# Five stage boundaries of a two-block transformer kernel without a meeting of all engines

## The chip, the cores and the metric

The kernel runs on one core of a Trainium2 chip. The metric is the device time of one launch in microseconds, the median over runs. Everything is float32.

## The reference, cut to what matters

512 tokens (four tiles of 128) of width 1024 go through two blocks. The first block mixes (gMLP, RG-LRU, HGRN2, pooling), then a convolved feed-forward, then a gated per-layer embedding. The second block has attention and routed experts, two layers of it.

```python
# first block, one layer (D_MODEL 1024, D_FF 2816)
h = rms_norm(x, norm1_g); z = h @ w_in; mix = concat(y_a, y_b, y_c, y_d)
x = x + mix @ w_out                                   # stage mix_out
hf = causal_dwconv(rms_norm(x, norm2_g) @ w_up)       # stage up
gt, val = split(hf)
x = x + (gelu(gt) * val) @ w_down                     # stage down
gate = sigmoid(rms_norm(x, norm3_g) @ w_pg)           # stage gate
x = rms_norm(x + (p @ w_pe) * gate, final_g)
# second block, two layers
x = layer_norm(ALPHA * x + mixer(x), ...)             # even_in, even_ab, even_out / odd_in ... odd_out
x = layer_norm(ALPHA * x + routed_moe(x), ...)        # route, experts, overflow, combine
```

## The kernel before, in words

The five engines run one list of 22 stages, `STAGES`. At the end of a stage each engine calls `meet()`: it drains, adds one to the semaphore `met` and waits until all four compute engines have done so. The stages named in `NO_MEET` (line 194) leave this out; before, those are the output projections, the routing and the experts of the second block. So the PE, DVE, ACT and POOL programs of every other stage start together. Semaphores for products and evacuations belong to a `Flow`; two of them take turns by the stage's parity, and POOL clears the one of the stage that ended.

Five of the stage ends that meet matter here: mix_out to up, up to down, down to gate, gate to even_in, combine0 to odd_in.

**Weights.** They come in pieces of up to 2 MB into `ring`, six slots, issued in order by SP. SP waits for `w_used`, which PE raises by `release()` when a piece has been used, so that the next five pieces are there or on the way. `product()` (line 579) is a chain of matmuls over the eight 128-row pieces of the contraction. Each float32 matmul of the program is two PE instructions in the trace, each with a weight load of its own, so a 128 x 512 product over the full width is 16 instructions.

**The end of an output stage** (mix_out, down, gate). PE computes two column halves for the four token tiles. DVE adds each into `x` (`residual()`), and after the second half of a tile it computes the norm's statistics (`norm_tile()`), with a square root by ACT, and writes the normalised tile. PE turns the tile, eight transposes of 128 x 128 (`turn_tile()`, line 586), into two PSUM banks, and the tile is copied from there into `xT`, the operand of the next stage: by DVE with a gain for mix_out and down (`take_tile`, line 1655), by ACT for gate (line 1211), by both for combine0 (`take`, lines 1257 and 2210). `turn_behind()` (line 606) turns a tile two products behind; after the last product three tiles are turned one after the other, and for mix_out and down tile 3 waits for the banks of tile 1. In combine(), all four turns come after the last product. DVE's order in `residual()` is: norm of tile 2, take tile 0, norm of tile 3, take tiles 1, 2, 3.

**The stages behind them.** `up()` (line 804) makes 44 feature products with `xT` (512 columns) as the moving operand; ACT scales each into `conv`, DVE adds the two other taps, and the last 22 are multiplied into `hidden`. `down()` (line 817) reads `hidden` as the stationary operand, six pieces, eight banks. `gate()` (line 836) makes for each tile and half a product with `pT` (4 instructions) and one with `xT` (16), in pairs of banks. `even_in()` (line 862) and `odd_in()` (line 1085) begin with feature products over all of `xT`.

**POOL.** In `up()` it clears the rows of `expert_rows` with 12 writes of 512 KB (line 2358) and waits for them; in `down()` it loads `pT`, in `gate()` the gain `final_g` and the pack for even_in; in `odd_in()` it clears halves of `kI`.

## Time and profile before

| | us |
|---|---|
| median of 3 timed runs | 2092.29 |
| lowest, highest | 2090.55, 2104.61 |
| the profiled execution | 2081.75 |
| its span on the core | 2080.1 |

The profile shows the profiled execution alone. Its span is the time from the first to the last instruction; 1.65 us lie around it. Start times in the rows below are microseconds from the start of the span. In the timeline a row is a run of like instructions: start, time that it covers, engine, line and operation, output and input with their sizes, count, and in brackets the idle time of the engine before it with what ended it.

### The profile page before, as it was taken

The page shows a single profiled execution, that of the slowest core. Times are in us where ns is not written, and L with a number is a line of the kernel's source. Part 1 is how long each engine was busy: PE and PEld are TensorE (multiplying, and loading weights), DVE is VectorE, ACT ScalarE, POOL GpSimd, SP SyncE. Part 2 cuts the span into 40 slices and gives each one's busy share as a digit, 9 for nine tenths or more (in the row PEclk, how much of TensorE's full clock was granted, in tenths as well). Part 3 has the DMA queues.
Part 4 walks back from the last instruction along what each step waited for, and adds up shares of the span by engine and source line. Part 5 has one row for each costly group of instructions (what it writes and reads, how often), then busy time and mean ns, then how long its engine had stood idle before and what let it go on. Part 6 is the DMA issues. An engine that isn't in the chain of part 4 may idle for free.

```text
span 2080.1 us, 23209 instructions
## 1 busy us (share of the span) xinstructions
PE 1960.8 (94%) x9718; PEld 886.6 (43%) x9718; DVE 671.1 (32%) x1600; ACT 401.1 (19%) x869; POOL 82.3 (4%) x106
## 2 busy tenths in 40 slices
PE   6999999999999998999996999998999898899997
PEld 3464444444444444444644333333645445333332
DVE  3746322223300033014725100005686645300005
ACT  3203011111100003103701111112116431111112
POOL 0000010000000000000000200010000000200001
PEclk9989999999999999999996999999898998899999
DMA  4203552211221113101044899992110234599994
GB/s 151 71 21 103 199 203 81 74 51 67 81 81 61 61 54 121 64 18 41 1 162 148 310 424 414 416 388 114 41 41 1 81 122 162 171 415 417 420 412 188
DMA packets 71001, 335.56 MB, mean 161 GB/s; under 512 B 4536, under 2 KB 12744, under 8 KB 58480
## 3 DMA queue, kind: packets, MB, share of 16 engines
q1 hardware_dynamic: 56752, 283.80, 35.4%
q0 software_dynamic: 10976, 37.76, 4.8%
q10 hardware_dynamic: 3168, 12.50, 1.5%
q8 instruction: 78, 1.28, 0.2%
q14 instruction: 27, 0.22, 0.0%
HBM read 310.94 MB, written 23.09 MB: 161 GB/s over the span
## 4 chain that ended last, share of the span: by engine, by line
PE 90%; DVE 5%; ACT 2%; issue 1%; DMA 1%; DVEq 0%; another core or an unknown queue 0%; ACTq 0%; SPq 0%
PE psum L582 39%; PE psum L983 24%; PE psum L825 7%; PE psum L762 4%; PE psum L894 3%; PE psum L923 2%; PE psum L907 2%; PE psum L965 1%; PE psum L1078 1%; PE psum L1009 1%; PE psum L704 1%; PE psum L594 1%; ACT ring L1436 1%; PE psum L1101 0%; PE psum L658 0%
## 5 line engine op out<-in xcount | busy, mean ns | idle before, releaser
L983 PE MATMUL psum<-ring,scratch 128*32 128x512 f32 x3840 | 507.8, 598 | 2.9 <-DVE scratch L2139 1.6
L582 PE MATMUL psum<-xT,ring 128*128 128x512 f32 (+2 forms) x1056 | 466.0, 602 | 8.6 <-PE psum L582 3.4
L582 PEld LDWEIGHTS psum<-xT,ring 128*128 128x128 f32 (+2 forms) x1056 | 199.7, 191 | 272.4 <-issue 271.5
L983 PEld LDWEIGHTS psum<-ring,scratch 128*32 128x32 f32 x3840 | 140.6, 111 | 285.0 <-issue 276.5
L582 PE MATMUL psum<-ring,xT 128*128 128x512 f32 (+4 forms) x704 | 242.6, 501 | 2.5 <-ACTq L1187 1.6
L582 PEld LDWEIGHTS psum<-ring,xT 128*128 128x128 f32 x704 | 123.1, 199 | 120.1 <-issue 111.9
L825 PE MATMUL psum<-ring,scratch 128*128 128x512 f32 x352 | 155.7, 603 | 4.0 <-remote 3.3
L1600 DVE SCALAR_TENSOR_TENSOR scratch<-psum,overlay,scratch 128x511 f32<-128x511 f32 x88 | 65.9, 749 | 232.2 <-ACT scratch L1366 230.6
L983 PE MATMUL psum<-xT,scratch 128*32 128x512 f32 x768 | 127.0, 593 | 0.0
L2137 DVE TENSOR_TENSOR scratch<-psum,scratch 128x512 f32<-128x512 f32 x24 | 16.6, 692 | 309.9 <-PE psum L983 309.9
L825 PEld LDWEIGHTS psum<-ring,scratch 128*128 128x128 f32 x352 | 67.4, 193 | 91.6 <-issue 91.6
L762 PE MATMUL psum<-xT,ring 128*128 128x512 f32 x224 | 101.6, 609 | 2.5 <-DVEq L1589 2.3
L1600 DVE SCALAR_TENSOR_TENSOR x<-x,psum 128x512 f32<-128x512 f32 x32 | 22.0, 688 | 234.7 <-PE psum L825 141.3
L1366 ACT ACTIVATE scratch<-psum,overlay 128x512 f32<-128x512 f32 x44 | 34.2, 778 | 269.5 <-PE psum L582 269.5
L582 PE MATMUL psum<-ring,scratch 128*128 128x512 f32 x160 | 72.6, 606 | 3.0 <-DVEq L1589 1.6
L2139 DVE COPY scratch<-psum 128x512 f32<-128x512 f32 x24 | 16.6, 692 | 179.8 <-PE psum L1009 179.8
L894 PE MATMUL psum<-scratch 64*128 64x256 f32 (+11 forms) x256 | 68.1, 483 | 4.0 <-DVEq L1589 1.8
L1424 ACT ACTIVATE ring<-ring,small 128x257 f32<-128x257 f32 (+5 forms) x128 | 68.1, 540 | 6.3 <-DVE small L1990 6.3
L1210 ACT ACTIVATE small<-small 128x1 f32<-128x1 f32 x20 | 4.1, 203 | 337.5 <-DVE small L1636 337.5
L762 PEld LDWEIGHTS psum<-xT,ring 128*128 128x128 f32 x224 | 43.5, 196 | 55.5 <-issue 55.2
L1458 ACT ACTIVATE scratch<-psum 128x512 f32<-128x512 f32 x48 | 26.3, 595 | 191.5 <-PE psum L965 191.5
L1483 ACT ACTIVATE scratch<-psum 128x512 f32<-128x512 f32 x48 | 28.7, 597 | 155.7 <-PE psum L983 155.7
(374 smaller groups left out, 1667.1 us busy)
## 6 DMA issues: line engine op xcount, KB each, us to landing
ring<-in_moe_w_gate SPq DMA_DIRECT2D x28, 2048.0 KB, 11.0
ring<-in_moe_w_up SPq DMA_DIRECT2D x28, 2048.0 KB, 13.6
ring<-in_moe_w_down SPq DMA_DIRECT2D x24, 2048.0 KB, 12.4
ring<-in_w_up SPq DMA_DIRECT2D x11, 2048.0 KB, 7.9
xT<-in_moe_w_down SPq DMA_DIRECT2D x8, 2048.0 KB, 11.6
expert_rows<-scratch ACTq DMA_DIRECT2D x20, 512.0 KB, 10.9
ring<-in_w_down SPq DMA_DIRECT2D x4, 2048.0 KB, 7.7
ring<-in_even_w_in SPq DMA_DIRECT2D x4, 2048.0 KB, 7.7
```

What stands on the lines that cost most here:

```text
L582: mm = nc.tensor.matmul(out_, lhsT, rhs, start=(j == 0), stop=(j == len(pairs) - 1))
L762: mm = nc.tensor.matmul(banks[k % 2][:, :], lhsT, rhs, start=(t == 0), stop=(t == KD - 1))
L825: mm = nc.tensor.matmul(banks[4 * half_ + n][:, :], hidden[:, k0 + t, n * P:(n + 1) * P], w_[:, t, :], start=(k0 + t == 0), stop=(k0 + t = ...
L894: mm = nc.tensor.matmul(banks[2 * (p % 2) + hh][:, 0:span(kind, n)[1]], head_q(kind, n, j, hh), head_k(kind, n, j, hh), start=True, stop=True)
L907: mm = nc.tensor.transpose(banks[4 + u % 2][:, b * P:(b + 1) * P], probs[:, u % 6, b * P:(b + 1) * P], ident)
L923: mm = nc.tensor.matmul(banks[6 + g % 2][r, c], head_v(kind, s0 // P + b, h), probsT[:, (2 * p + hh) % 4, b * P:(b + 1) * P], start=(b == ...
L983: mm = nc.tensor.matmul(bank[r, :], lhsT[:, t, r], w_[:, t, c0:c0 + 512], start=(t == 0), stop=(t == nk - 1))
L1366: A(conv[:, k % 4, :], banks[k % 8][:, :], ACT.Identity, bias=operand["fconv_b"][:, k:k + 1], scale=w3[:, k, 2:3]).then_inc(f.a, 1)
L1424: A(to, of, ACT.Exp, bias=negmax[:, u % 8:u % 8 + 1], accum_out=p_total[:, u % 8:u % 8 + 1])\
L1458: A(xgT[:, 4 * h:4 * h + 4, :].rearrange("p a b -> p (a b)"), banks[h][:, :], ACT.Copy).then_inc(xgT_ready, 1)
L1483: A(y_sb[:, g % 2, j * 512:(j + 1) * 512], banks[5 + j][:, :], ACT.Copy).then_inc(y_taken, 1)
L1600: return V.scalar_tensor_tensor(out_, in0, s, in1, ALU.mult, ALU.add)
```

## The change

The five stages mix_out, up, down, gate and combine0 join `NO_MEET`, so there is no meeting at the five boundaries. Data waits take its place:

- The output stages share one product counter `out_mm` and one evacuation counter `out_used` with base values; gate has counters of its own; `Flow`s are given to five stages, and POOL clears them after norm1 and even_in.
- At the three boundaries into feature products (up, even_in, odd_in), the last tile is turned no longer by the stage before. A new function `enter_features()` waits for tiles 0 to 2, multiplies their 384 columns for the first feature, turns tile 3, multiplies the 384 columns for the second feature, waits for tile 3, and then multiplies the remaining 128 columns for both.
- gate waits for each tile when it needs it, uses the banks in a rotated order (`gate_bank`: 4, 6, 0, 2), and turns the last tile of down after its first pair of products.
- down waits for the eviction of up's last banks bank by bank and for `hidden` piece by piece (`val_scaled`).
- POOL's steps of these stages run as soon as their own waits allow: the clearing writes of up() right after the meeting of mixers, the load of `pT` behind them. `final_g` waits for down's last product, the pack for even_in for the last tile taken, the clearing of `kI` for the last product of combine0.
- The expert pieces count in `w_loaded` instead of semaphores of their own (not shown). Sizes and order of the loads stay as they are.

```diff
@@ -191,7 +191,7 @@
-NO_MEET = ("even_out", "route0", "experts0", "overflow0", "odd_out", "route1", "experts1", "overflow1")
+NO_MEET = ("mix_out", "up", "down", "gate", "combine0", "even_out", "route0", "experts0", "overflow0", "odd_out", "route1", "experts1", "overflow1")
@@ -279,7 +280,14 @@
                 self.mm, self.a, self.v, self.s = (sem(f"{name}_{m}") for m in ("mm", "act", "dve", "stats"))
         turns = [Flow("even_stage"), Flow("odd_stage")]
-        flow = {s: turns[i % 2] for i, s in enumerate(STAGES)}
+        flow = {"norm1": turns[0], "up": turns[1], "even_in": turns[0], "odd_in": turns[1], "latent": turns[0]}
+        done_with = {"norm1": turns[0:1], "even_in": turns}
+        gate_mm, gate_opened, gate_used = sem("gate_mm"), sem("gate_opened"), sem("gate_used")
+        out_mm, out_used = sem("out_mm"), sem("out_used")
+        OUT_MM = {"mix_out": 0, "down": 8, "even_out": 32, "odd_out": 40}
+        OUT_USED = {"mix_out": 0, "down": 8, "even_out": 16, "odd_out": 24}
...
         late_w, late_mm, late_ready, late_done = sem("late_w"), sem("late_mm"), sem("late_ready"), sem("late_done")
+        late_taken = sem("late_taken")
         early_added, over_known, moe_rows = sem("early_added"), sem("over_known"), sem("moe_rows")
@@ -470,7 +482,14 @@
         def turn_bank(stage, n):
-            return 2 * n if stage in ("gate", "combine0") else 2 * (n % 2)
+            if stage == "gate":
+                return gate_bank(n)
+            return 2 * n if stage == "combine0" else 2 * (n % 2)
+        def gate_bank(i):
+            return (2 * i + 4) % 8
         keys_cleared = sem("keys_cleared")
         listed = sem("listed")
@@ -610,10 +629,34 @@
                 if n == NT - 1:
                     route_tile(stage, n - 3)
                     turn_tile(stage, n - 1)
+                    if stage in ("mix_out", "down", "gate"):
+                        return
                     route_tile(stage, n - 2)
                     route_tile(stage, n - 1)
                     turn_tile(stage, n)
                     route_tile(stage, n)
+            def tile_there(stage, n):
+                pe.wait_ge(tile_taken, norm_base[stage] + n + 1)
+                if stage == "combine0":
+                    pe.wait_ge(late_taken, n + 1)
+            def enter_features(behind, f, columns):
+                def part(k, q):
+                    w_, c0, m = columns[k]
+                    return product(banks[k][0:m, q], [(w_[:, t, c0:c0 + m], xT[:, t, q]) for t in range(KD)])
+                early, last = slice(0, (NT - 1) * P), slice((NT - 1) * P, T)
+                tile_there(behind, NT - 2)
+                part(0, early)
+                turn_tile(behind, NT - 1)
+                part(1, early)
+                tile_there(behind, NT - 1)
+                for k in range(2):
+                    part(k, last).then_inc(f.mm, 1)
@@ -783,20 +826,19 @@
             def halves(name, chunk_name, lhs):
-                f = F[name]
                 for half_, (at, c) in enumerate(by_name[chunk_name]):
                     arrived(at)
                     w_ = slot_view(at, c)
                     for n in range(NT):
                         k = NT * half_ + n
                         product(banks[k][:, :], [(lhs[:, t, n * P:(n + 1) * P], w_[:, t, :]) for t in range(KD)])\
-                            .then_inc(f.mm, 1)
+                            .then_inc(out_mm, 1)
                         if half_ == 1:
                             if n == NT - 1:
@@ -806,7 +848,9 @@
                 for j, (at, c) in enumerate(by_name["w_up"]):
                     arrived(at)
                     w_ = slot_view(at, c)
-                    for g in range(4):
+                    if j == 0:
+                        enter_features("mix_out", f, [(w_, g * P, P) for g in range(2)])
+                    for g in range(0 if j else 2, 4):
                         k = 4 * j + g
                         if k >= 8:
@@ -815,25 +859,27 @@
                     release(f.mm, 4 * j + 4)
             def down():
-                f = F["down"]
                 for j, (at, c) in enumerate(by_name["w_down"]):
                     arrived(at)
                     w_ = slot_view(at, c)
                     half_, k0 = j // 3, c[1]
+                    pe.wait_ge(val_scaled, k0 + c[2])
                     for n in range(NT):
+                        if j == 0:
+                            pe.wait_ge(F["up"].v, 2 * FT - 3 + n)
                         for t in range(c[2]):
                             mm = nc.tensor.matmul(banks[4 * half_ + n][:, :], hidden[:, k0 + t, n * P:(n + 1) * P],
                                                   w_[:, t, :], start=(k0 + t == 0), stop=(k0 + t == FT - 1))
-                        mm.then_inc(f.mm, 1)
+                        mm.then_inc(out_mm, 1)
...
                         if j == 5:
                             if n == NT - 1:
-                                release(f.mm, NT * 6)
+                                release(out_mm, OUT_MM["down"] + NT * 6)
                             turn_behind("down", n)
                     if j < 5:
-                        release(f.mm, NT * (j + 1))
+                        release(out_mm, OUT_MM["down"] + NT * (j + 1))
             def gate():
-                f = F["gate"]
@@ -842,34 +888,41 @@
                     arrived(at)
                     w_g = slot_view(at, c)
                     for n in range(NT):
-                        k = 2 * (NT * half_ + n)
-                        bank_emptied(f, "va" * 8, k)
-                        product(banks[k % 8][:, :], [(pT[:, t, n * P:(n + 1) * P],
-                                                      w_e[:, t, half_ * 512:(half_ + 1) * 512]) for t in range(2)])\
-                            .then_inc(f.mm, 1)
-                        bank_emptied(f, "va" * 8, k + 1)
-                        product(banks[(k + 1) % 8][:, :], [(xT[:, t, n * P:(n + 1) * P], w_g[:, t, :]) for t in range(KD)])\
-                            .then_inc(f.mm, 1)
+                        i = NT * half_ + n
+                        if half_ == 0:
+                            tile_there("down", n)
+                        else:
+                            pe.wait_ge(gate_used, i - NT + 1)
+                        product(banks[gate_bank(i)][:, :], [(pT[:, t, n * P:(n + 1) * P],
+                                                             w_e[:, t, half_ * 512:(half_ + 1) * 512]) for t in range(2)])
+                        product(banks[gate_bank(i) + 1][:, :], [(xT[:, t, n * P:(n + 1) * P], w_g[:, t, :]) for t in range(KD)])\
+                            .then_inc(gate_mm, 1)
+                        if i == 0:
+                            turn_tile("down", NT - 1)
                         if half_ == 1:
                             if n == NT - 1:
-                                release(f.mm, 16)
-                                release(f.mm, 16)
+                                release(gate_mm, 8)
+                                release(gate_mm, 8)
                             turn_behind("gate", n)
                     if half_ == 0:
-                        release(f.mm, 8)
+                        release(gate_mm, NT)
             def even_in():
                 f, k = F["even_in"], 0
                 pe.wait_ge(pack_loaded["even"], 16)
                 for j, (at, c) in enumerate(by_name["even_w_in_2"]):
                     arrived(at)
+                    if j == 0:
...
+                        enter_features("gate", f, [(slot_view(at, c), g * P, P) for g in range(2)])
+                        k = 2
                     if j == 1:
                         bank_emptied(f, EVEN_IN, k)
                         product(banks[k % 8][0:8, :], [(fg_w[:, t, :], xT[:, t, :]) for t in range(KD)]).then_inc(f.mm, 1)
                         k += 1
                         features(f, EVEN_IN, k, at, c, 0)
                         k += 1
-                    for g in range(4):
+                    for g in range(0 if j else 2, 4):
@@ -1079,7 +1132,7 @@
                                                   y_sb[:, g, h * 512:(h + 1) * 512], start=(g == 0), stop=(g == 1))
                     mm.then_inc(late_done, 1)
                 if l == 0:
-                    for n in range(NT):
+                    for n in range(NT - 1):
                         turn_tile("combine0", n)
             def odd_in():
@@ -1087,8 +1140,8 @@
                 (a0, c0), (a1_, c1), (a2, c2) = by_name["odd_w_in_2"]
                 pe.wait_ge(pack_loaded["odd"], 16)
                 arrived(a0)
-                features(f, ODD_IN, 0, a0, c0, 384, HD)
-                features(f, ODD_IN, 1, a0, c0, P)
+                w_ = slot_view(a0, c0)
+                enter_features("combine0", f, [(w_, 384, HD), (w_, P, P)])
                 features(f, ODD_IN, 2, a0, c0, 2 * P)
                 for n in range(NT):
@@ -1663,16 +1714,15 @@
             def residual(name, scale, loads=0, first=None):
-                f = F[name]
                 for k in range(10):
                     if first and k < NT:
                         first(k)
                     if k < 8:
-                        dve.wait_ge(f.mm, (20 if k >= 4 else 8) + k % 4 + 1 if name == "down" else k + 1)
+                        dve.wait_ge(out_mm, OUT_MM[name] + ((20 if k >= 4 else 8) + k % 4 + 1 if name == "down" else k + 1))
                         r = x[:, k % 4, (k // 4) * 512:(k // 4 + 1) * 512]
-                        mul_add(r, r, scale, banks[k][:, :]).then_inc(f.v, 1)
+                        mul_add(r, r, scale, banks[k][:, :]).then_inc(out_used, 1)
                         if k >= 4:
@@ -2210,8 +2259,9 @@
                 def take(n):
                     dve.wait_ge(tile_turned, base + n + 1)
                     for k in range(KD // 2, KD):
-                        V.tensor_scalar(xT[:, k, n * P:(n + 1) * P], banks[2 * n + 1][:, (k - 4) * P:(k - 3) * P],
-                                        operand["moe_g"][:, k:k + 1], operand["moe_b"][:, k:k + 1], ALU.mult, ALU.add)
+                        ins = V.tensor_scalar(xT[:, k, n * P:(n + 1) * P], banks[2 * n + 1][:, (k - 4) * P:(k - 3) * P],
+                                              operand["moe_g"][:, k:k + 1], operand["moe_b"][:, k:k + 1], ALU.mult, ALU.add)
+                    ins.then_inc(late_taken, 1)
                 for n in range(NT + 2):
@@ -2330,13 +2380,12 @@
             steps = [2]
-            def meet(i):
+            def meet(stage):
                 meets[0] += 1
                 pool.drain().then_inc(met, 1)
                 pool.wait_ge(met, 4 * meets[0])
                 pool.drain()
-                if i >= 0:
-                    f = turns[i % 2]
+                for f in done_with.get(stage, ()):
                     for s in (f.mm, f.a, f.v, f.s):
                         pool.sem_clear(s)
@@ -2375,7 +2424,10 @@
                 pool.dma_start(pT.rearrange("p t q -> p (t q)"), w["pT"]).then_inc(pT_loaded, 16)
             def gate():
+                pool.wait_ge(out_mm, OUT_MM["down"] + 24)
                 pool.dma_start(rowsG, w["final_g"]).then_inc(rows_loaded, 16)
+                pool.wait_ge(tile_taken, norm_base["down"] + NT)
                 pool.dma_start(pack_area["even"], w["pack_even"]).then_inc(pack_loaded["even"], 16)
             def clear_halves(tiles):
@@ -2390,6 +2442,8 @@
                 pool.dma_start(kB[HD:HD + 1, :, :], negc[0:8, :]).then_inc(bias_row, 16)
             def odd_in():
+                pool.wait_ge(late_done, NT)
                 clear_halves(kI)
```

## Rows read from the trace of the kernel before

**Rows 1.** The page's first part and its clock row.

```profile
PE 1960.8 (94%) x9718; PEld 886.6 (43%) x9718; DVE 671.1 (32%) x1600; ACT 401.1 (19%) x869; POOL 82.3 (4%) x106
...
PEclk9989999999999999999996999999898998899999
```

**Rows 2.** The chain of work that ended last, shares of the span by engine.

```profile
PE 90%; DVE 5%; ACT 2%; issue 1%; DMA 1%; DVEq 0%; another core or an unknown queue 0%; ACTq 0%; SPq 0%
```

**Rows 3.** Pieces of that chain in order: start us, us, what, instructions.

```profile
577.71 3.27 another core or an unknown queue
580.98 30.79 PE psum L825 x64
611.91 27.72 PE psum L825 x64
...
746.63 36.75 PE psum L582 x80
```

**Rows 4.** Stretches: busy us (instructions) of each engine, granted clock, DMA share, GB/s.

```profile
578.00:580.00 2.00, 0.00 (x0) 0.00 (x0) 1.40 (x2) 0.53 (x1) 0.00 (x0) 1.00 0.47 87
...
582.00:584.00 2.00, 2.00 (x4) 0.97 (x3) 0.00 (x0) 0.23 (x1) 0.27 (x1) 0.50 1.15 375
...
588.00:590.00 2.00, 2.00 (x6) 0.94 (x5) 0.00 (x0) 0.00 (x0) 0.00 (x0) 1.00 0.03 8
```

**Rows 5.** Timeline, mix_out to up.

```profile
259.07 1.94 PE L594 MATMUL psum<-base,scratch 128*128 128x128 f32 x16
...
262.93 3.82 DVE L1659 TENSOR_TENSOR xT<-psum,overlay 128x512 f32<-128x512 f32 x6
...
266.90 2.07 PE L582 MATMUL psum<-xT,ring 128*128 128x512 f32 x2 [1.48 <-DVEq L1589]
```

**Rows 6.** Timeline, up to down.

```profile
580.13 0.69 DVE L1922 TENSOR_TENSOR scratch<-scratch 128x512 f32<-128x512 f32 x1
```

**Rows 7.** Timeline, down to gate.

```profile
738.32 1.94 PE L594 MATMUL psum<-base,scratch 128*128 128x128 f32 x16
...
745.07 1.29 DVE L1659 TENSOR_TENSOR xT<-psum,overlay 128x512 f32<-128x512 f32 x2 [0.41 <-PE psum L594]
...
746.63 3.75 PE L582 MATMUL psum<-ring,scratch 128*128 128x512 f32 x4 [1.60 <-DVEq L1589]
```

**Rows 8.** Timeline, gate to even_in.

```profile
819.45 1.94 PE L594 MATMUL psum<-base,x 128*128 128x128 f32 x16 [0.30 <-PE psum L582]
...
823.52 2.04 ACT L1215 ACTIVATE xT<-psum 128x512 f32<-128x512 f32 x4
...
827.85 4.61 PE L582 MATMUL psum<-xT,ring 128*128 128x512 f32 x5 [1.38 <-ACTq L1187]
```

**Rows 9.** Timeline, combine0 to odd_in.

```profile
1429.23 1.09 PE L594 MATMUL psum<-base,x 128*128 128x128 f32 x8 [2.83 <-DVE x L2205]
...
1429.77 2.88 ACT L1261 ACTIVATE xT<-psum,base 128x128 f32<-128x128 f32 x8
...
1435.19 5.35 PE L582 MATMUL psum<-xT,ring 128*64 128x512 f32 x6 [1.80 <-ACTq L1187]
```

**Rows 10.** Timeline, transposes between products, and products of 128 columns.

```profile
251.02 1.04 PE L594 MATMUL psum<-base,scratch 128*128 128x128 f32 x8
...
251.89 7.03 PE L582 MATMUL psum<-ring,scratch 128*128 128x512 f32 x16
...
872.14 7.31 PE L582 MATMUL psum<-ring,xT 128*128 128x128 f32 x64
```

**Rows 11.** The page's costliest groups: busy, mean ns of one, idle before.

```profile
L582 PEld LDWEIGHTS psum<-ring,xT 128*128 128x128 f32 x704 | 123.1, 199 | 120.1 <-issue 111.9
```

**Rows 12.** Timeline of SP's issues, and stretches of mix_out with columns as in Rows 4.

```profile
202.38 95.82 SPq L2525 DMA_DIRECT2D ring<-in_w_up  x7
...
210.00:220.00 10.00, 10.00 (x25) 4.42 (x24) 1.00 (x2) 0.00 (x0) 0.00 (x0) 1.00 1.05 387
...
240.00:250.00 10.00, 10.00 (x25) 4.42 (x24) 4.77 (x12) 0.41 (x2) 0.00 (x0) 1.00 0.00 0
```

40 lines of the change are left out of this document (20 added, 20 removed).

## The prediction

> **What bounds the kernel now.** I read the page's busy shares first. TensorE is busy for 1960.8 of 2080.1 us, and its clock row stands at 9 or nearly 9 everywhere except in a few slices [rows 1]. The chain of work that ended last says the same from the other side: 90% of it is PE [rows 2]. So only time in which PE stands still, or runs at the lower level of its clock, can be won, and a faster DVE or DMA is worth nothing by itself. The next view is the same chain in order of time, because there a hole in PE's work shows as a piece that is not PE. At the end of up there is such a hole of 3.27 us, and the 64 instructions behind it take 30.79 us, while the next 64, of the same kind, take 27.72 [rows 3]. The third view, stretches of 2 us, tells why: granted clock 1.00 while PE stands still, 0.50 from 582 to 584, 1.00 again from 588 [rows 4]. That is 2.4 GHz, then 1.2 GHz, then 2.4 GHz. A hole therefore costs twice, once as idle time and once as slow work behind it. The last view is the timeline of each of the five boundaries, to see what PE waits for [rows 5 to 9].
>
> **What the meetings cost themselves.** Almost nothing. Before up, DVE's last copy into xT ends at 262.93 + 3.82 = 266.75, and PE starts at 266.90: 0.15 us [rows 5]. Before gate it is 746.63 - (745.07 + 1.29) = 0.27 us [rows 7]. So the gain is not five meetings, it is what PE can do before the last tile of xT exists. This has to be counted boundary by boundary. The unit prices: one full instruction 27.72 / 64 = 0.433 us [rows 3]; one of 384 columns 0.75 of it, 0.325; one of 128 columns 7.31 / 64 = 0.114 [rows 10]; eight transposes between products 251.89 - 251.02 = 0.87 us [rows 10].
>
> **1. up to down.** PE is idle from 577.71 to 580.98. ACT and DVE work in it on up's last feature; the last step, the product into hidden, ends at 580.13 + 0.69 = 580.82 [rows 6]. After the change down's first piece needs features 0 to 7 of hidden and the banks of features 40 to 43, one by one; the last of those banks is asked for after three groups of 16 instructions, 21 us later, and the last feature only in the third piece. So PE goes on after the usual step between pieces, 611.91 - (580.98 + 30.79) = 0.14 us [rows 3]. Gain 3.27 - 0.14 = 3.13, and without a hole the clock has no reason to fall: 30.79 - 27.72 = 3.07. Together **6.20 us**. The cover of ACT's and DVE's tail is down's first 21 us; without it, it costs again the 3.1.
>
> **2. down to gate.** The transposes of tiles 1 and 2 end at 738.32 + 1.94 = 740.26; gate begins at 746.63 [rows 7]. After the change gate's first pair (4 + 16 instructions, 8.7 us) needs only tile 0, which has been taken long before, and banks 4 and 5, emptied long before. It starts at 740.26 + 0.15. Tile 3's transposes follow it, at about 749, when its banks have long been free; its copy (1.3 us) ends before the fourth pair asks for it, 17 us later. DVE waits for those transposes with its gate work queued behind them, but the first sigmoid is there only at 749 as well, and the pairs leave 8.7 us for each. Gain 746.63 - 740.41 = 6.22, less 0.87 for transposes that now stand in the line of work: 5.35. The 80 instructions from 746.63 took 36.75 us, at the full clock 80 x 0.433 = 34.65 [rows 3]: 2.10 more. Together **7.45 us**.
>
> **3. mix_out to up.** PE can start when tile 2 is taken, but DVE takes tiles 1, 2, 3 in one go of 3.82 us, 1.27 each, after the norm of tile 3. Tile 2 is there at 262.93 + 2.55 = 265.48, so PE starts at 265.63 and wins 1.27 us, no more. It now carries tile 3's transposes itself: 0.87. The two features cost 32 x 0.325 + 32 x 0.114 = 14.05 us instead of 32 x 0.433 = 13.86: 0.19. DVE's copy of tile 3 lies beside the second 384-column part (5.2 us). PE's idle stretch from 261.01 to 265.63 is no shorter than before, so I leave the slow stretch behind it as it is. Left: **0.21 us**.
>
> **4. gate to even_in.** The same with ACT taking the tiles: tiles 1 and 2 are there at 823.52 + 2.04 = 825.56, PE starts at 825.71 instead of 827.85 [rows 8]. 2.14 - 0.87 - 0.19 = **1.08 us**, slow stretch kept.
>
> **5. combine0 to odd_in.** Tiles 1 and 2 are taken at 1429.77 + 2.88 = 1432.65, start at 1432.80 instead of 1435.19 [rows 9]: 2.39 - 0.87 - 0.19 = **1.33 us**, slow stretch kept.
>
> **What I cost at nothing.** The counters out_mm and gate_mm replace others one for one. POOL's pT, final_g and even_in pack are asked for by POOL as soon as their places are free, and each is needed tens of us later. Clearing kI moves from odd_in into combine0, beside DVE's chain there; at worst two memsets' worth, about 1 us. The clearing writes, 12 x 512 KB = 6.3 MB, move from up to mix_out, past the w_up pieces that SP has queued from 202.38. There the DMA engines moved 387 GB/s from 210 to 220 and nothing from 240 to 250 [rows 12]. 6.3 MB at 387 GB/s are 16 us and end by about 250, before up asks for its first piece at 265.6. The Trainium skill (Trainium Kernel Development and Optimization, Key Constraints) says that transfers from SP's, ACT's and POOL's queues run on the same 16 DMA engines and interleave; so moving these writes would not be free of the loads. The row of 210 to 220 with share 1.05 agrees that nothing is to spare there; by the rule alone the sum stays the same as long as the idle stretch behind it holds both.
>
> **The sum.** 6.20 + 7.45 + 0.21 + 1.08 + 1.33 = 16.3 us. Against the profiled execution: 2081.75 - 16.3 = 2065.5. That execution lies 0.5% under the median of the timed runs, 2092.29, and a gain of a fixed number of us should not depend on it, so the forecast is 2092.3 - 16.3 = **2076.0 us**, 0.8% less.
>
> **Unknown costs, from both sides.** (a) The slow stretch at boundaries 3 to 5. Where it can be read it cost 2.10 and 3.07 us [rows 3]. It may vanish at all three (up to 3 x 3.07 = 9.2 more gain) or catch tile 3's transposes and a longer part (about 1 us more at each). The Trainium skill (TensorE: Matmul & The Clock Gate, Part 1) says that the same kernel has differing numbers of slow matmuls from run to run; that is a reason for a range and gives no other sum. (b) The 3 x 32 = 96 narrow instructions. The nearest row has a stationary operand of the same size and 128 columns, 0.114 us [rows 10]; the other bound is the length of a weight load, 199 ns [rows 11], should it not hide under so short a matmul: 96 x 0.085 = 8.2 more. I take 0.114, because weights are loaded in that row as well. (c) The median of three runs: the runs of before lie 14 us apart, so a median may be off by 6 to 8.
>
> **Rivals.**
> - *The clock doesn't fall at boundaries 3 to 5 any more.* For it: two of the three holes get shorter. Against: the transposes that broke the hole before are now behind it, so the hole in one piece is longer at boundary 3 (4.6 us against 3.2, from 261.01 to the copy of tile 1 at 264.20). Gain 16.3 + 9.2 = 25.5: 2066.8 us. Chance 0.12.
> - *The narrow pieces are bound by their weight loads*, as in (b): gain 8.1, 2084.2 us. Against: 64 such instructions in a row at 0.114. Chance 0.08.
> - *The clock still falls at boundaries 1 and 2*, for instance because the step between stages is longer than thought: gain 16.3 - 5.2 = 11.1, 2081.2 us. Chance 0.05.
> - *The change does not do what it says*: the gain is given back later, where loads and not PE set the pace, in the experts' stages. For it: the DMA share there is high. Against: PE is 90% of the chain over the whole span, and the loads wait for PE's releases. 2091 us. Chance 0.04.
> - *Slower: the clearing writes hold up the weights.* Place: mix_out, where 6.3 MB of writes share the engines with the second w_out piece and the first w_up piece, 4.2 MB. Those 10.5 MB must be through by 265.6, 63 us after 202.4: 166 GB/s suffice, 387 were seen. Each us later costs PE one. It decides from 80 us on, that is below 131 GB/s, where the delay eats the 16.3; at a quarter of the measured rate, 97 GB/s, the writes end at 310.6, 45 us late: 2121 us. Chance 0.03.
> - The forecast: 0.68.
>
> **The range.** 2065 to 2088: down to the first rival, up past the second and third, with the spread of a median of three on either side. What a measurement of this kernel can tell from no change is about 1%, 21 us: below 2071.4 or above 2113.2. Faster by that: the first rival, and of the forecast, whose centre is 4.6 us short of the bound, about a fifth: 0.12 + 0.13 = 0.25. Slower by it: the last rival, 0.03. The rest is 0.72.
>
> **What would show it.** Step 1: no hole at the end of up, down's first 64 instructions in 27.7 us, granted clock 1.00 throughout. Step 2: the first gate product within 0.3 us of the transposes, 80 instructions and 8 transposes in 35.5 us. Steps 3 to 5: PE starts right after tile 2's copy, and the 32 narrow instructions take 3.7 us. For the last rival: PE waiting for DMA in mix_out or up. The prediction is wrong if the clock falls in a place where PE had no hole, if the narrow instructions take over 0.15 us each, or if any stage behind shows an idle time of PE that it had not before.

## The result, and the profile after

| | us |
|---|---|
| kernel before, median of 4 runs (lowest, highest) | 2095.91 (2090.55, 2104.61) |
| changed kernel, median of 4 runs (lowest, highest) | 2074.22 (2069.86, 2079.25) |
| ratio after / before, 95% interval | 0.9893 [0.9849, 0.9937] |
| profiled execution, before and after | 2081.75, 2074.65 |
| span, before and after | 2080.1, 2073.0 |

The forecast was 2076.0. The medians differ by 21.7 us, the two profiled executions only by 7.1. Both differences have to be explained; neither is the 16.3 of the sum. The forecast took its start from a median of three runs of the kernel before, 2092.3; with the fourth run beside the result it is 2095.9.

The page after, its first part and its clock row, answers to [rows 1], and its chain by engine to [rows 2].

```profile
PE 1960.0 (95%) x9814; PEld 895.2 (43%) x9814; DVE 670.9 (32%) x1600; ACT 401.0 (19%) x869; POOL 82.1 (4%) x106
...
PEclk9989999999999999999996999999989997999999
...
PE 91%; DVE 4%; ACT 2%; issue 1%; DMA 1%; DVEq 0%; SPq 0%; ACTq 0%
```

96 more PE instructions, as counted; PE is still the bound. The page is too coarse for a gain of 1%, so I went to the chain of the changed kernel in order of time: start us, us, what, instructions.

```profile
265.52 7.09 PE psum L601 x16
272.61 0.87 PE psum L613 x8
273.48 22.48 PE psum L601 x80
...
548.20 27.72 PE psum L601 x64
576.21 27.72 PE psum L872 x64
604.22 27.72 PE psum L872 x64
...
731.26 1.94 PE psum L613 x16
733.20 8.59 PE psum L601 x20
741.78 0.87 PE psum L613 x8
742.66 25.77 PE psum L601 x60
...
808.62 1.95 ACT xT L1268 x4
810.71 7.92 PE psum L601 x16
```

Against [rows 3]: between up's last 64 instructions, which end at 575.92, and down's first at 576.21 only a step of 0.29 us is left, and down's first 64 instructions take 27.72 instead of 30.79. From down's transposes (731.26) to gate (733.20) there is no hole either; tile 3's eight transposes stand behind the first 20 instructions. At the entry of up and of even_in the first piece of 16 is one of 384 columns. The stretches of 2 us answer to [rows 4] (busy us and instructions of PE, PEld, DVE, ACT, POOL; granted clock; DMA share; GB/s).

```profile
262.00:264.00 2.00, 0.00 (x0) 0.00 (x0) 1.94 (x4) 0.00 (x0) 0.00 (x0) 1.00 1.04 404
...
266.00:268.00 2.00, 2.00 (x5) 1.08 (x4) 0.00 (x0) 0.00 (x0) 0.00 (x0) 0.57 0.04 11
268.00:270.00 2.00, 2.00 (x5) 1.14 (x4) 0.00 (x0) 0.00 (x0) 0.00 (x0) 0.58 0.00 0
270.00:272.00 2.00, 2.00 (x8) 1.20 (x7) 0.00 (x0) 0.00 (x0) 0.00 (x0) 1.00 0.00 0
...
578.00:580.00 2.00, 2.00 (x6) 0.95 (x5) 0.98 (x2) 0.02 (x1) 0.00 (x0) 1.00 0.99 354
580.00:582.00 2.00, 2.00 (x6) 0.90 (x5) 0.00 (x0) 0.00 (x0) 0.00 (x0) 1.00 0.98 377
```

At up to down the clock stays at 2.4 GHz; at mix_out to up it still falls to 1.2 GHz, with the hole that was left there.

**The stretch table.** To compare many profiles I took the starts of PE's instructions in each trace and the time between fixed ones: from mix_out's first product to up's third feature (A), from there to down's second piece (B), from there to the second half of gate (C), from there to even_in's third feature (D), and from combine0's first product to odd_in's third feature (E). Each holds exactly one of the five boundaries. The last column is the rest, from odd_in's third feature to the end. The rows are all profiles of the two kernels; the padded ones are described below.

| us | A | B | C | D | E | rest |
|---|---|---|---|---|---|---|
| before | 81.35 | 328.10 | 171.79 | 60.47 | 41.12 | 628.30 |
| before_again | 79.66 | 326.68 | 171.75 | 60.46 | 41.39 | 631.47 |
| before_third | 81.31 | 328.07 | 171.76 | 60.46 | 40.24 | 638.94 |
| before_p192 (padded) | 80.83 | 324.98 | 172.89 | 60.74 | 41.41 | 631.51 |
| before_route (padded) | 82.09 | 327.99 | 171.75 | 60.47 | 38.37 | 629.85 |
| mean | 81.05 | 327.16 | 171.99 | 60.52 | 40.51 | |
| after | 79.62 | 322.17 | 164.49 | 59.37 | 39.72 | 633.21 |
| after_again | 79.62 | 322.16 | 164.49 | 59.34 | 39.82 | 626.68 |
| after_third | 79.62 | 322.17 | 164.50 | 59.35 | 39.33 | 630.81 |
| after_p64 (padded) | 80.29 | 322.20 | 164.50 | 59.32 | 39.84 | 626.69 |
| after_p128 (padded) | 80.76 | 322.19 | 164.55 | 59.54 | 39.76 | 626.70 |
| after_route64 (padded) | 79.62 | 322.19 | 164.49 | 59.30 | 39.31 | 626.26 |
| mean | 79.92 | 322.18 | 164.50 | 59.37 | 39.63 | |
| first pair's gain | 1.73 | 5.93 | 7.30 | 1.10 | 1.40 | -4.91 |
| gain of the means | 1.13 | 4.98 | 7.49 | 1.15 | 0.88 | |
| the prediction | 0.21 | 6.20 | 7.45 | 1.08 | 1.33 | |

What lies ahead of A and between D and E, where PE's instructions are the same in both kernels, is not in the table. The five stretches gained 1.73 + 5.93 + 7.30 + 1.10 + 1.40 = 17.5 us in the first pair and 15.6 in the means; the sum of the prediction was 16.3. B and C lie clear of the spread of either kernel, and so does D. A and E do not: before_again has an A of 79.66 and before_route an E of 38.37. What remains is why the first pair shows 7.1 and the medians about 20.

### The profile page after: what moved, and what is told of

Read it like the earlier page. It is cut to its first block, busy times and chain, and to the rows that moved or that the text cites. A ratio compares the mean times of both kernels' runs of the same rounds, so it can differ in the third digit from the quotient of the medians.

```text
span 2073.0 us, 23327 instructions
## 1 busy us (share of the span) xinstructions
PE 1960.0 (95%) x9814; PEld 895.2 (43%) x9814; DVE 670.9 (32%) x1600; ACT 401.0 (19%) x869; POOL 82.1 (4%) x106
## 4 chain that ended last, share of the span: by engine, by line
PE 91%; DVE 4%; ACT 2%; issue 1%; DMA 1%; DVEq 0%; SPq 0%; ACTq 0%
PE psum L601 39%; PE psum L1036 25%; PE psum L872 7%; PE psum L805 5%; PE psum L947 3%; PE psum L976 2%; PE psum L960 2%; PE psum L1018 1%; PE psum L1131 1%; PE psum L1062 1%; PE psum L747 1%; PE psum L613 1%; ACT ring L1487 1%; PE psum L1154 0%; PE psum L701 0%
## 5 line engine op out<-in xcount | busy, mean ns | idle before, releaser
L1036 PE MATMUL psum<-ring,scratch 128*32 128x512 f32 x3840 | 518.4, 598 | 5.3 <-DVE scratch L2188 1.6
L601 PE MATMUL psum<-xT,ring 128*128 128x512 f32 (+5 forms) x1152 | 465.3, 564 | 15.3 <-DVE xT L1710 4.5
L601 PEld LDWEIGHTS psum<-xT,ring 128*128 128x128 f32 (+2 forms) x1152 | 210.1, 190 | 266.1 <-issue 257.1
L872 PE MATMUL psum<-ring,scratch 128*128 128x512 f32 x352 | 152.7, 593 | 1.8 <-PE psum L872 1.5
L601 PE MATMUL psum<-ring,scratch 128*128 128x512 f32 x160 | 70.7, 594 | 1.3 <-ACTq L1240 0.9
## 6 DMA issues: line engine op xcount, KB each, us to landing
ring<-in_moe_w_gate SPq DMA_DIRECT2D x28, 2048.0 KB, 10.9
```

The lines of the kernel that those rows point to most:

```text
L601: mm = nc.tensor.matmul(out_, lhsT, rhs, start=(j == 0), stop=(j == len(pairs) - 1))
L872: mm = nc.tensor.matmul(banks[4 * half_ + n][:, :], hidden[:, k0 + t, n * P:(n + 1) * P], w_[:, t, :], start=(k0 + t == 0), stop=(k0 + t = ...
L1036: mm = nc.tensor.matmul(bank[r, :], lhsT[:, t, r], w_[:, t, c0:c0 + 512], start=(t == 0), stop=(t == nk - 1))
```

## The experiments

There are three sets of runs, each with its own runs of the kernel before beside it on one chip. The theory was that the five stretches give the gain, by PE's work in the holes and by the clock behind the two that close. One rival was that the missing meetings give it by themselves. Another was that part of the gain is given back in the experts' stages, as the first profile after seemed to show.

### What the first profile gave back

This is a piece of the chain of the changed kernel in the experts' stage of the first layer, 128 instructions of hidden products.

```profile
1137.90 7.67 PE psum L1036 x64
1145.57 0.39 issue
1145.96 1.31 PE psum L1036 x4
1147.27 0.12 issue
1147.39 7.07 PE psum L1036 x60
1154.46 1.09 PE psum L1018 x8
```

The 128 instructions take 1154.46 - 1137.90 = 16.56 us, and PE waits for nothing that the profile shows. The four at 1145.96 take 0.33 us each instead of 0.11, and the granted clock is 1.00 (stretches, columns as before):

```profile
1146.00:1148.00 2.00, 1.88 (x12) 0.47 (x15) 0.00 (x0) 0.37 (x1) 0.00 (x0) 1.00 0.01 0
1148.00:1150.00 2.00, 2.00 (x24) 0.69 (x18) 0.00 (x0) 0.22 (x1) 1.56 (x2) 1.00 0.94 82
```

There are two such places in each layer's experts. By PE's starts the same instructions take 2.7, 3.8, 2.7 and 3.8 us more than in before, 13.0 together. That is what the first pair gave back: 17.5 less 13.0, and 2.6 won elsewhere by the clock, make 7.1. Two things lay near the places in that profile: a train of eight indexed transfers that POOL issues one after the other, and a boundary between two pieces in which PE's program is fetched (the page's instruction queue for it moves 79 packets after, 78 before). The change moves PE's instructions against these pieces, so my theory was that it had brought a boundary into the train of transfers. Waits that hold at once, put into PE's program, shift the boundaries.

```diff
+            for _ in range(128):      # after_p64: 64 more PE instructions; after_p128: 256 waits, 128;
+                pe.wait_ge(root_set, 1)   # before_p192: 384 waits, 192. All ahead of the first stage
             for s in stages:
```

> The changed kernel with 64 more semaphore instructions at the very start of PE's program (a wait on root_set that is long fulfilled), where PE waits for x anyway, so that they cost nothing themselves. The change made PE's program 192 instructions longer in front of the experts, and PE's program is fetched in pieces of 256 instructions (16 KB packets of the instruction queue); 64 more bring the edges of these pieces back to where they were before. Theory 1, that the four slow places of PE in the experts' stages (together about 13 us in the profile of the changed kernel) come from piece edges that fall late into POOL's train of eight indirect DMAs: the four places are gone, the span is 2073.0 - 13 = 2060. Rival, that they come from the changed times or from the new semaphores: they stay, 2073.

> The kernel before with 192 more semaphore instructions at the start of PE's program, under 10 us at 0.05 us each, while PE waits until 13 us for x: by themselves about nothing. They put the edges of PE's instruction pieces where the changed kernel has them. Theory 1: the four slow places appear, 2080.1 + 13 = 2093 span, about 0.6% slower than the kernel before. Rival: no change, ratio 1.000 within 0.3%.

> The changed kernel with 128 more semaphore instructions at the start of PE's program. The edges of the pieces come 128 instructions, about 7 us in the experts' stages, earlier than in the changed kernel, so just ahead of the start of POOL's trains or 1 us into them. Theory 1: no slow place in the experts' first groups, span about 2060 to 2066. Rival: 2073.

> The kernel before, unchanged, for a second profile. If its timed runs (2090 to 2105) differ from its profiled one (2081.75) by slow places that come and go, this profile shows some of them; if the profile again gives about 2080 without slow places in the experts, the difference lies elsewhere. Both theories: ratio 1.00.

Measured: after_p64 2065.03 us, ratio 0.9905 [0.9885, 0.9925]; after_p128 2065.64, 0.9923 [0.9901, 0.9944]; before_p192 2095.02, 1.0044 [1.0026, 1.0063]; before_again 2082.54, 1.0006 [0.9992, 1.002]. The slow places were gone in both padded versions of after, but they did not appear in before_p192. It is slower for another reason: its padding is not hidden. PE starts at 21.93 instead of 13.17 us, 8.8 later, and the mixers take 193.0 instead of 189.3. So I moved the padding to a place where PE waits anyway, the routing, and ran the changed kernel again without any.

```diff
+                for _ in range((128, 0)[l]):      # after_route64, ahead of the wait for the choice, layer l
+                    pe.wait_ge(root_set, 1)       # before_route: 160 and 96 in layer 0, 128 in layer 1
```

> The changed kernel, unchanged, beside the others of this chip. Theory 1 (the places of PE's instruction stream decide over the slow places in the experts' stages): the four slow places are there again, first distance of the hidden products 19.8 us instead of 17.2 and last distance 25 instead of 22.64 in both layers, ratio 0.9965 (7 us less). Rival (they come and go by chance): no or other slow places, ratio 0.992.

> The changed kernel with 64 more semaphore instructions of PE (3.3 us) in route0, where PE waits 6.2 us for DVE's choice. So nothing in front of the experts changes, neither instructions nor times. Theory 1: the slow places are gone in both layers, 2073.0 - 12.9 = 2060 span, ratio to the kernel before 0.990 to 0.992, which beats both kernels. Rival: same as the changed kernel, slow places stay.

> The kernel before with 128 more semaphore instructions of PE in route0 (80 where it waits 6.2 us, 48 where it waits 2.9 us) and 64 in route1: exactly so many that the pieces of PE's program end at the same instructions of both experts' stages as in the changed kernel, with the times in front as before. They cost under 1 us. Theory 1: slow places appear in the experts' stages, up to 13 us, ratio 1.006. If the clock time of the edges relative to other traffic matters as well: only some, 1.001 to 1.005. Rival: none, 1.000.

Measured: after_again 2065.12 us, 0.9902 [0.9873, 0.9932]; after_route64 2061.23, 0.9893 [0.9872, 0.9914]; before_route 2084.49, 0.9997 [0.998, 1.0014]. The theory fell. after_again is the changed kernel with nothing altered, and the same 128 instructions stand in one piece:

```profile
1143.29 13.87 PE psum L1036 x128
1157.15 1.09 PE psum L1018 x8
```

13.87 us instead of 16.56. The boundaries of its program are those of the first profile. And before_route, padded so that its pieces meet the train as in after, has no slow place. A last pair of profiles, on one chip, settled whose they are.

> The changed kernel once more, beside the two versions above and the kernel before on one chip. If the net gain is the sum of the five stretches (15 to 17 us) and what the clock does in odd_in and odd_d (2 to 6 us), the ratio is 0.990 to 0.992. The slow places of PE in the experts' stages, 2 to 3 us each, four in the first profile of this kernel and none in the second: if they belong to the program, they are here again; if they come and go between executions, there is no reason to expect any. After odd_in's third feature 626.7 us without them, 633 with four.

> The kernel before, one more profile. Two things were seen in only one of two profiles of it: the stretch at the lower clock behind up's hole, 6.8 us or less (stretch to down's second piece 328.1 or 326.7), and a stretch of 10.2 us at the lower clock in odd_d, costing 4.7 us, which its first profile lacks and the later ones have. If the first is a matter of the execution, the stretch lies between 325 and 328.5; if the second is the rule for this kernel, odd_in's third feature to the end is 631.5, else 628.3.

Measured: after_third 2073.23 us, ratio 0.9918 [0.9886, 0.995]; before_third, a single run, 2096.0 beside a median of 2090.7. Both have slow places, at the same four points of the work: 1.7, 3.6, 1.7 and 2.9 us in before_third, 1.8, 2.7, 1.7 and 2.8 in after_third. The chain of before_third at the first:

```profile
1159.93 2.14 PE psum L983 x18
1162.07 0.10 issue
1162.17 1.06 PE psum L983 x5
1163.23 0.37 issue
1163.60 6.22 PE psum L983 x53
```

The same row of after_third is 0.36 issue between 5 and 54 instructions. The distance from DVE's step on this expert's hidden product to its step on the next is 18.91 us in before_third and 18.93 in after_third, against 17.20 in the profiles without a slow place and 19.86 in the first profile after. The two versions of the next part, profiled on the same chip, have 18.91 and 18.90. So the slow places are a matter of the chip or the moment, not of the change: all four profiles of this set have them, of four different programs, and of the ten others only the first profile after. What they lie next to can be read from the same traces. The first indexed transfer and the slow place behind it stand as follows (us): after 1135.94 and 1145.57, after_third 1138.44 and 1148.25, before_third 1152.26 and 1162.07, 9.6, 9.8 and 9.8 apart, at the eighth transfer of the train.

```profile
1152.26 1.01 POOL L2416 DMA_INDIRECT expert_tokens<-token_id,place  x1 [17.18 <-PE psum L965]
...
1161.31 0.97 POOL L2416 DMA_INDIRECT expert_tokens<-token_id,place  x1 [0.30 <-issue]
```

The nearest packet of PE's program is no such mark: it comes 4.0 us ahead of the place in before_third (1158.1), and 4.3 us behind it in after_third (1152.6). So a fixed distance to the fetching of PE's program is out. The distance to POOL's train does not prove the train, though. A product of PE releases it, and in all fourteen profiles the same instructions of PE run beside it. What sets the five apart is when the train lands. POOL's next transfer waits for it, in after and in after_again:

```profile
1148.14 1.02 POOL L2473 DMA_DIRECT2D idx_sb<-expert_tokens  x1 [2.19 <-DMA expert_tokens<-token_id,place]
```

```profile
1160.90 1.02 POOL L2473 DMA_DIRECT2D idx_sb<-expert_tokens  x1 [9.57 <-DMA expert_tokens<-token_id,place]
```

In both layers this wait is 2.2 to 5.8 us in the five profiles with slow places and 8.7 to 10.9 in the nine without. The slow places thus come with a train that lands sooner. Which of the two brings the other, or what third thing brings both, stays open.

### Each boundary by itself

```diff
-NO_MEET = ("even_out", "route0", "experts0", "overflow0", "odd_out", "route1", "experts1", "overflow1")
+NO_MEET = ("up", "even_out", "route0", "experts0", "overflow0", "odd_out", "route1", "experts1", "overflow1")
...
             def down():
                 f = F["down"]
+                pe.wait_ge(pool_step, 1)
...
+                    pe.wait_ge(val_scaled, k0 + c[2])
                     for n in range(NT):
+                        if j == 0:
+                            pe.wait_ge(F["up"].v, 2 * FT - 3 + n)
```

This is before_up, the kernel before with the one meeting of up taken away and the data waits of the change in its place, and one wait for POOL's first step; gate's counters start from where up's end (not shown).

> The kernel before with the meeting between up and down alone taken away (with the waits that the change puts into down, and one wait of PE on POOL's first step). My sum: 3.13 us of idle time and 3.07 us of slow clock go, 6.2 us in this stretch. By trace after the change this stretch gained 5.9. Rival, that the join pays only together with the others: 0 to 3. The program is shorter or longer by a few instructions only, so no slow places in the experts' stages: ratio 0.997.

Measured: 2083.2 us, 0.9995 [0.9977, 1.0012]. The stretches: A 79.67, B 322.27, C 172.40, D 60.47, E 41.38, rest 631.55. B is within 0.1 us of the changed kernel's; the others, but for C, are those of before. Its stretches of 2 us at the boundary, and its chain:

```profile
576.00:578.00 2.00, 1.61 (x4) 0.87 (x5) 1.14 (x2) 1.97 (x2) 0.00 (x0) 1.00 0.31 61
578.00:580.00 2.00, 2.00 (x6) 0.86 (x5) 1.05 (x2) 0.09 (x1) 0.00 (x0) 1.00 1.01 336
```

```profile
576.39 27.72 PE psum L829 x64
604.11 0.29 issue
604.40 27.72 PE psum L829 x64
```

So step 1 stands alone: hole and slow stretch go with this one meeting. C is 0.6 longer than in before, because each later piece of down carries a second wait, and the step between pieces is 0.29 us instead of 0.14. Against the mean of before, B is 4.9 shorter. So the profile leads one to expect 4.9 - 0.6 = 4.3 us less than the kernel before; the ratio gives 1 us less with an interval from 4.8 us less to 2.5 more. So the gain of this step is shown in the profile and not in the timed runs.

```diff
 # after_gate_late, in gate(): tile 3 turned and awaited before the first pair, not behind it
                         i = NT * half_ + n
+                        if i == 0:
+                            turn_tile("down", NT - 1)
+                            tile_there("down", NT - 1)
                         if half_ == 0:
...
-                        if i == 0:
-                            turn_tile("down", NT - 1)
```

> The changed kernel with one step moved: tile 3 of down's output is turned and awaited before gate's first pair of products and not behind it, without a meeting. Theory (step 2): what is won there is PE's work in the hole, so the hole comes back, 5.35 us, and with it a stretch at the lower clock, about 2.1 us: the stretch from down's second piece to gate's second half goes from 164.5 to about 171.8 us, the kernel is 7.4 us slower than the changed one. Rival: the meeting itself was the cost; then 164.5 stays within 0.5 us. A third case, hole without slow clock: 169.9. All expect the other stretches unchanged (79.6, 322.2, 59.3, 39.8).

Measured: 2083.19 us, 0.9969 [0.9952, 0.9985]; beside after_third on the same chip 10.0 us slower. The stretches: A 80.28, B 322.17, C 172.33, D 58.54, E 39.25, rest 630.24. C is 7.83 longer, the size of step 2, with no meeting in it. The chain and the clock say how:

```profile
741.33 1.32 PE psum L613 x8
...
744.02 36.99 PE psum L601 x80
```

```profile
742.00:744.00 2.00, 0.64 (x4) 0.24 (x2) 1.67 (x3) 0.00 (x0) 0.00 (x0) 0.50 1.04 392
```

The hole is back, the clock falls to 1.2 GHz while it lasts, and the 80 instructions take 36.99, as in [rows 3]. The rival, that the meeting itself was the cost, is out for this boundary. D got 0.8 shorter: its slow stretch is 3.4 us instead of 6.8.

```diff
 # after_whole, in enter_features(): all 512 columns of both features after tile 3
-                early, last = slice(0, (NT - 1) * P), slice((NT - 1) * P, T)
-                tile_there(behind, NT - 2)
-                part(0, early)
                 turn_tile(behind, NT - 1)
-                part(1, early)
                 tile_there(behind, NT - 1)
                 for k in range(2):
-                    part(k, last).then_inc(f.mm, 1)
+                    part(k, slice(0, T)).then_inc(f.mm, 1)
```

> The changed kernel with the split of the first two features undone at the three boundaries into feature products: tile 3 is turned first, and then both features are multiplied over all 512 columns. No meeting comes back. If steps 3 to 5 of the prediction have the right cause (PE starts before the last tile is there), the stretches return to those of before less the 0.15 us of the meeting: mix_out to up's third feature 79.6 -> about 81.2 us (the slow stretch behind the hole as long as before, 6.8 instead of 3.4 us), gate to even_in's 59.3 -> 60.3, combine0 to odd_in's 39.7 -> 41.2; together 3.5 to 4.2 us slower than the changed kernel, 2.6 if only the starts count and the clock gives nothing. The rival, that the missing meetings and not the split gave these gains, expects 79.6, 59.4 and 39.8 to stay within 0.3 us each. Both expect up to down (322.2) and down to gate (164.5) unchanged.

Measured: 2076.1 us, 0.9921 [0.9897, 0.9945]. The stretches: A 80.79, B 322.16, C 164.49, D 61.63, E 41.06, rest 632.46. A, D and E are 1.17, 2.28 and 1.73 longer than in after_third, 5.2 us together; the medians differ by 2.9, less than their intervals can tell. So the split is what gives the gain of step 4, and most likely that of step 5: without it D is even 1.1 longer than before, and E is as long as in most profiles of before. For step 3 this run shows nothing, because with the split A can be as long (80.76 in after_p128). The chain at even_in shows why.

```profile
815.23 1.95 PE psum L613 x8
...
818.34 30.79 PE psum L601 x64
```

The eight transposes in the middle of the hole ran at the lower clock already, 1.95 us where eight take 0.87 in the line of work, and the 64 instructions that begin at 818.34 are slow for another 30.79 - 27.72 = 3.07 us. The granted clock is at its lower level from 814.3 on, for 10.2 us, against 6.8 in before.

## Why the prediction was right

**The reading that PE sets the time** held: 91% of the chain, and every gain is one in PE's starts.

**1. up to down: 6.20 forecast.** 5.93 in the first pair, and B is between 322.16 and 322.27 in every profile that has it, before_up among them. The 0.27 missing are two steps of 0.29 instead of 0.14 between pieces, which carry a wait more. The term that was mis-sized is the slow stretch: over five profiles of before, B lies between 324.98 and 328.10, since that stretch lasts from nothing to 6.8 us. What the meeting cost is thus 2.8 to 5.9 us, with a mean of 5.0. I had read 3.07 from one profile as if it were a constant.

**2. down to gate: 7.45 forecast.** 7.30, and 7.5 in the means. The first 88 instructions of gate take 8.59 + 0.87 + 25.77 = 35.2 us, 35.5 was forecast. The four steps between pieces of down lose about 0.6, which I had not put in the sum, and the hole and the clock gave about 0.5 more. Undone by itself it cost 7.83.

**3. mix_out to up: 0.21 forecast.** PE starts at 265.52, forecast 265.63 [rows 5]. But the stretch gained 1.73 in the first pair, because the slow stretch shrank from 6.8 to 3.4 us: my assumption that it stays as it is failed there. It fails in both directions, since two profiles of before (79.66, and 79.67 of before_up) have the short one too, and two of after the long one. In before_route it is even 10.2 us. Where both kernels have the short one, A is 79.66 before and 79.62 after. The gain of the means is 1.1, and no run shows what part of it is the change's.

**4 and 5. gate to even_in and combine0 to odd_in: 1.08 and 1.33 forecast.** 1.10 and 1.40, and 1.1 and 0.9 in the means. PE starts at 810.71, right after ACT's copy of tile 2; timelines of after, with what [rows 8] and [rows 9] show of before:

```profile
808.53 2.04 ACT L1268 ACTIVATE xT<-psum 128x512 f32<-128x512 f32 x4
...
810.71 7.92 PE L601 MATMUL psum<-xT,ring 128*128 128x384 f32 x16 [4.31 <-ACT xT L1268]
...
1422.30 7.58 PE L601 MATMUL psum<-xT,ring 128*64 128x384 f32 x16 [2.58 <-DVE xT L2262]
```

16 instructions of 384 columns should take 5.2 us; 7.92 and 7.58 say that the slow stretch is still there. At even_in it is as long as assumed, 6.8 us in both kernels. At odd_in it is not: it lasts 10.2 us in before, from 1430.2, and 6.8 us in after, from 1420.0, as in all six profiles of the changed kernel. In after_whole it is 10.2 again. before_route alone has 3.4 there, which is why its E is the shortest of all. So the assumption of an unchanged slow stretch failed at steps 3 and 5 and held at step 4. The Trainium skill (TensorE: Matmul & The Clock Gate, Part 1) says that the number of slow matmuls differs from run to run. The table agrees, with B of before between 324.98 and 328.10 for work that is the same to the instruction.

**The unknown costs.** (b) The narrow instructions are not bound by their weight loads: the piece 273.48 22.48 x80 holds 32 full ones (13.86) and 16 of 384 columns (5.20), which leaves 3.42 for 32, 0.107 us each; the taken value was 0.114. (c) The medians: those of the kernel before were 2095.91, 2081.8, 2085.64 and 2090.7 in the four sets, of the changed one 2074.22, 2065.12 and 2073.23. A difference within a set is worth more than any of these, as the 14 us between them show.

**The signs of being wrong.** The third of them came true to the letter: in the first profile of the changed kernel PE idles 0.39 and 0.12 us inside the experts, where it had not before. The experiments showed that this is no effect of the change, so the sign was too sharp for a single pair of profiles.

**What was costed at nothing.** The clearing writes were through at 234.4, forecast 250 at the latest: POOL's load of `pT` waits for them.

```profile
203.73 6.55 POOL L2407 DMA_DIRECT2D expert_rows<-scratch  x12 [0.31 <-POOL scratch L2404]
...
234.37 0.54 POOL L2424 DMA_DIRECT2D scratch<-in_pT  x1 [22.98 <-DMA expert_rows<-scratch]
```

PE's wait at the entry of up ends with DVE's copy and not with a DMA, so the rival by which the writes hold up the weights is out.

**The sum, and the net.** The five stretches gave 15.6 to 17.5 for 16.3. The medians gave 21.7, 20.5 and 17.5. The 2 to 6 us above the 15.6 of the means come from stages that the change doesn't touch, and from the clock again. In odd_in, the first 100 instructions from the third feature on take 25.0 us in every profile of the changed kernel and 26.6 in three of five before. A later part of odd_in goes the other way: 120 instructions of it take 36.3 us (35.9 in two) after and 34.9 in three of five before. In odd_d, a later stage, 100 instructions take 22.3 us in every profile of after and 26.9 to 28.1 in four of five before; in those they lie partly at 1.2 GHz. Stretches of 10 us, of before_again and of after_again at the same place of the work:

```profile
1630.00:1640.00 10.00, 8.96 (x28) 3.73 (x27) 3.67 (x12) 3.29 (x7) 0.00 (x0) 1.00 0.48 169
1640.00:1650.00 10.00, 9.07 (x38) 5.86 (x37) 6.30 (x40) 5.71 (x29) 0.00 (x0) 0.59 0.42 177
...
```

```profile
1618.00:1628.00 10.00, 10.00 (x23) 3.22 (x21) 3.11 (x5) 4.73 (x8) 0.00 (x0) 1.00 0.58 210
1628.00:1638.00 10.00, 8.04 (x54) 5.62 (x54) 8.27 (x47) 6.78 (x32) 0.00 (x0) 1.00 0.58 212
```

The work is the same and PE pauses in both; the clock fell in one and not in the other. The first profile of before had no slow stretch there, which is why the first pair doesn't show this gain. Why an unchanged stage should keep the clock up is not settled: all eight profiles in which combine0's meeting is gone have it, and of the six others one. Over the profiles without slow places the rest is 626.6 us in the mean after and 630.3 before, and what lies between D and E 566.1 and 566.4. 15.6 + 3.7 + 0.3 = 19.6 us, which is between the medians' 17.5 and 21.7.

That 2074.2 lies only 1.8 us from the forecast of 2076.0 is in part luck. The kernel before turned out 3.6 us slower than the median that the forecast started from, and the change gained 5.4 us more than the sum. The sum itself was right in its mechanism and large terms; that 15.6 to 17.5 stand against 16.3 owes something to errors that cancel, the slow stretch at step 1 taken too long and that at steps 3 and 5 taken as fixed.

**The rivals.** That the clock no longer falls at boundaries 3 to 5: no, it falls at all three in every profile of the changed kernel. In the first pair it stays down for a shorter time at two of them, which accounts for most of the 1.5 us above the forecast at step 3. Slow narrow pieces: no. The clock still falls at 1 and 2: no, in none of the six profiles of the changed kernel. A gain given back in the experts: the first profile looked like it, and it was not of the change. A reader with only the first pair would have taken a loss of 13 us for real and missed a gain of 5.

## What to carry to other kernels

A meeting of engines cost 0.15 and 0.27 us by itself here; count what the bounding engine can do in the hole, and add what its clock loses behind it. Taking a meeting away where PE still waits for the last tile wins nothing, as after_whole shows at even_in. Before a difference of 0.5% is explained from two profiles, take a second one of each kernel: here one pair showed 7 us where three sets of timed runs show 17 to 22.

## What the runs showed of the hardware

- The slow stretch behind a hole is not of one length. It was 0 to 6.8 us at up to down, 3.4 or 6.8 (once 10.2) at mix_out to up, for the same hole. Eight transposes in the middle of the hole at even_in (after_whole) came with 10.2 us instead of 6.8. It also moves in stages far from the change.
- A second wait, one that holds at once, costs 0.15 us per step between pieces of down, where another wait is already there.
- PE can lose 1.7 to 3.9 us in one place at a granted clock of 1.00 and with no wait that the profile shows; it was in five of fourteen profiles, in both kernels, always in the experts' stages. The first place lies 9.6 to 9.8 us behind the first of eight indexed transfers of POOL, and in all five profiles these transfers land sooner than in the nine others: POOL waits 2.2 to 5.8 us for them instead of 8.7 to 10.9.
